# Earlier issue of ScalarE's last weight loads before each mixture-of-experts stage

## The reference

```
g_logits = h @ grp_w + grp_b                    # 4 groups
g_sel    = argmax(g_logits)
e_logits = (h @ exp_w + exp_b)[tok, g_sel]      # 8 experts of that group
e_p, e_i = top_k(softmax(e_logits), 2)
wts      = softmax(g_logits)[g_sel] * e_p / sum(e_p)
...
def run(tok, wt, e):                            # a block of up to 64 tokens of expert e
    xb  = h_pad[tok]
    hid = silu(xb @ w_gate[e]) * (xb @ w_up[e])
    return (hid @ w_down[e]) * wt
out = zeros.at[buf_tok].add(run over all blocks)
```

## Time and profile before

| | us |
|---|---|
| median of 3 runs | 2237.31 |
| lowest and highest run | 2236.52, 2237.57 |
| profiled execution | 2237.01 |
| its span, first to last instruction | 2235.2 |
| TensorE busy in the span | 2043.7 (91%) |
| VectorE, ScalarE, GpSimd busy | 851.1, 400.8, 239.3 |
| moved by DMA | 631.71 MB, mean 283 GB/s |

### The profile page before, as it was taken

One profiled execution on the slowest core, in us unless ns is written; L12 is line 12 of the kernel. 1 busy time (PEld: TensorE's weight loads), 2 busy tenths in 40 slices (PEclk: granted clock), 3 DMA queues, 4 the chain that ended last, 5 costly groups with the idle time before them and its releaser, 6 DMA issues.

```text
span 2235.2 us, 22516 instructions
## 1 busy us (share of the span) xinstructions
PE 2043.7 (91%) x8674; PEld 1067.4 (48%) x8674; DVE 851.1 (38%) x1698; ACT 400.8 (18%) x881; POOL 239.3 (11%) x303
## 2 busy tenths in 40 slices
PE   7989999999999999999988988989688898999985
PEld 3456666444766666445433333334355433434332
DVE  4756773464787126954210110101443311111111
ACT  2241000134100123653000000000343100000001
POOL 2010000000100003310121111111000111111110
PEclk9999999999999999999899999999899899999998
DMA  8865888343788612114899999999745799999996
GB/s 276 228 218 122 299 304 307 132 174 109 257 300 305 217 49 76 76 38 179 314 400 410 398 415 402 392 413 413 264 190 197 303 415 421 381 410 419 415 418 246
DMA packets 130835, 631.71 MB, mean 283 GB/s; under 512 B 16005, under 2 KB 18213, under 8 KB 104385
## 3 DMA queue, kind: packets, MB, share of 16 engines
q1 hardware_dynamic: 108064, 575.10, 65.5%
q0 software_dynamic: 19120, 33.31, 6.1%
q10 hardware_dynamic: 3568, 22.21, 2.6%
HBM read 625.46 MB, written 26.57 MB: 292 GB/s over the span
## 4 chain that ended last, share of the span: by engine, by line
PE 68%; DMA 23%; DVE 5%; ACT 2%; issue 2%; SPq 1%; ACTq 0%; DVEq 0%; POOLq 0%
DMA ring<-ex_up 20%; PE PS L1570 15%; PE PS L1243 10%; PE PS L1232 9%; PE PS L692 6%; PE PS L1170 6%; PE PS L1588 4%; PE PS L595 3%; PE PS L1560 2%; DMA ring<-a_w_qkv 2%; PE PS L2527 2%; PE PS L1028 1%; PE PS L1044 1%; PE PS L1208 1%; PE PS L2558 1%
## 5 line engine op out<-in xcount | busy, mean ns | idle before, releaser
L1570 PE MATMUL PS<-ring,arena 128*64 128x512 f32 x976 | 474.1, 643 | 83.6 <-DMA ring<-ex_up 81.7
L1573 PE MATMUL PS<-ring,arena 128*64 128x512 f32 x992 | 481.8, 643 | 0.0
L1570 PEld LDWEIGHTS PS<-ring,arena 128*64 128x64 f32 x976 | 138.7, 148 | 355.5 <-issue 329.0
L1900 DVE COPY arena<-PS 128x512 f32<-128x512 f32 x64 | 44.3, 692 | 616.3 <-PE PS L1560 616.3
L1588 PE MATMUL PS<-ring,arena 128*64 128x512 f32 x1008 | 230.1, 598 | 1.6 <-DVE arena L1896 1.6
L1243 PE MATMUL PS<-ring,arena 128*128 128x512 f32 x512 | 222.6, 592 | 0.0
L1232 PE MATMUL PS<-arena,ring 128*128 128x256 f32 x896 | 196.9, 380 | 0.0
L1232 PEld LDWEIGHTS PS<-arena,ring 128*128 128x128 f32 x896 | 169.3, 190 | 32.6 <-issue 10.1
L1243 PEld LDWEIGHTS PS<-ring,arena 128*128 128x128 f32 x512 | 97.0, 190 | 115.1 <-issue 114.3
L1702 ACT ACTIVATE arena<-PS 64x512 f32<-64x512 f32 x65 | 38.2, 588 | 610.2 <-PE PS L1570 578.3
L1983 POOL DMA_INDIRECT arena<-tokens_d,arena x65 | 62.4, 959 | 737.1 <-PE PS L1560 553.4
(11 more groups left out here) (317 smaller groups left out, 2245.9 us busy)
## 6 DMA issues: line engine op xcount, KB each, us to landing
ring<-ex_down SPq DMA_DIRECT2D x63, 2048.0 KB, 22.6
ring<-ex_up SPq DMA_DIRECT2D x62, 2048.0 KB, 22.4
ring<-ex_gate SPq DMA_DIRECT2D x61, 2048.0 KB, 17.5
ring<-ffn_w SPq DMA_DIRECT2D x32, 2048.0 KB, 12.9
ring<-mod_w SPq DMA_DIRECT2D x24, 2048.0 KB, 9.9
ring<-a_w_qkv SPq DMA_DIRECT2D x8, 2048.0 KB, 31.5
ring<-b_w_qkv SPq DMA_DIRECT2D x6, 2048.0 KB, 9.8
ring<-w_in_ab SPq DMA_DIRECT2D x3, 2048.0 KB, 8.8
```

The lines of the kernel that those rows point to most:

```text
L1570: g = pe.matmul(PS[0:CAP, u, :], xT[:, k, :], gate[k], start=(k == 0), stop=(k == KD - 1))
L1573: h = pe.matmul(PS[CAP:P, u, :], xT[:, k, :], up[k], start=(k == 0), stop=(k == KD - 1))
```

## The change

ScalarE's load of down_a is issued at the head of `act_moe`, once the logits are done (the turned tokens have been read by then, since ScalarE has copied the last of them). The other loads stay behind the exponents, but wait for the token stores and no longer for the two gathers.

```diff
         def act_moe(act, m, after=None):
             s, b0, T = m.s, m.b, m.tiles
+            act.wait_ge(s.logits, b0.logits + T)
+            spare_load(act, m, "down_a", 0)
             act.wait_ge(s.group_top, b0.group_top + 1)
 ...
             act.sem_inc(s.y_copied, 2)
             for u in range(2):
-                act.wait_ge(s.gathered[u], b0.gathered0 + 16)
-            spare_load(act, m, "down_a", 0)
+                act.wait_ge(s.token_stored[u], b0.token_stored0 + 16 * (T // 2))
             spare_load(act, m, "gate_c", 1)
             if m.l == 0:
                 spare_load(act, m, "gate_a", 1)
```

## The result

The changed kernel takes 2246.18 us (median of 7 runs, 2242.6 to 2252.56), the kernel before 2237.57 (7 runs, 2236.38 to 2239.53). The ratio is 1.0032, with a 95% interval of 1.0017 to 1.0048: slower by some 7 to 9 us. Run once more beside other kernels it gave 2246.30 and a ratio of 1.0040 [1.0024, 1.0057]. The forecast was 2238.1, in a range up to 2242.0. The profiled execution took 2247.5 us with a span of 2245.7; it is one of the slower half, so pieces of it can sum to a little more than the medians differ by.

The account below looks back on a forecast made before the run. The mixtures were taken as bound by DMA bytes, but the time here as set by TensorE's start on expert 0. Bytes, queue and clock at 0 and the first gather's +1.05 us on 2237.01 gave 2238.1 us, range 2235.4 to 2242.0.

Parts of the forecast that it names:

- The bytes: Loads of 3.67 MB and 3.15 MB move into the DMA hole before expert 0; nothing stood behind them: 0 us.
- The first rival: DMA short from the mixture stage's start, so every byte moved into the hole counts: 16.7 us faster, 2220.3 us; chance 0.05.
- ScalarE's queue: down_a's issue moves ahead of the exponents, which end 0.4 us later; later waits cover it: 0 us.
- The first gather: Expert 0's token gather, slowed beside the early loads by 2.05 us: TensorE late by +0.15 and +0.9 us in the layers.
- the slack: Time from the first gather's landing to TensorE wanting it before expert 0: 1.9 us and 1.1 us.
- the halving: Half of the third gather's extra 4.1 us taken for the first gather, as gate_c's packets are 8.3 KB, down_a's 16.3 KB.
- an upper bound of 5.3: First gather takes the third gather's full 7.0 us: TensorE starts 2.2 and 3.1 us late, +5.3 us.
- A gather cannot wait for a queue that is empty: Argument against the slower rival: the early loads' last data end at 1069.8 and 1745.9.
- The clock: TensorE's granted clock around expert 0: its start moves by less than a microsecond, so 0 us.
- My bound of 2.4 us in a layer: Five more pairs of expert 0's gate and up matmuls at the lower clock: +2.4 us in a layer.
- The slower rival: At `tokens_in(0, 0)` in both layers TensorE waits for a first gather of 7.0 us: +5.3 us, 2242.3 us; chance 0.07.

Follow-up runs that it names:

- run 6: Kernel before with the three loads issued only behind the first silu, in the part bound by DMA: 2251.55 us, ratio 1.0065.
- runs 1 and 2: Against the kernel before, only down_a issued early (1: 2240.31 us, ratio 1.0006) or only the gate parts early (2: 2238.22 us, ratio 0.9987).
- Run 8: Kernel before with down_a issued behind the exponents and token stores, the gate parts still behind the first two gathers: 2241.04 us, ratio 1.0021.
- run 11: Changed kernel with 6 keep-awake matmuls instead of 3 ahead of expert 0, and three more in expert 0's two waits: 2240.24 us, ratio 1.0018 to the kernel before.
- run 5: Changed kernel with 6 keep-awake matmuls instead of 3 ahead of expert 0: 2243.52 us, ratio 1.0024 to the kernel before.
- run 12: The whole change measured once more, unaltered, beside the kernel before: 2246.30 us, ratio 1.0040.

## Why the prediction was wrong

*The bytes: right.* They went into the hole, left one behind, and brought nothing. That the bound stretch is dear is shown by run 6 (+14.5 us), and that the old place was free by runs 1 and 2 (no clear gain). The first rival, 2220 us, is out.

*ScalarE's queue: right.* The exponents came 0.5 us later behind the last store in both layers, where I had 0.4, and no wait in these traces goes back to that.

*The first gather: the step that failed.* I had a measured size for it, 4.1 us beside the same three loads, and halved it, because the packets beside it would be half as large. The place, the slack and the direction were right, the halving was not. It landed in 6.4 and 7.2 us instead of 5.0 and 4.9, and TensorE's turn of tokens came 1.6 and 3.3 us late, 4.9 in sum, where I had 1.05 and an upper bound of 5.3. Run 8 shows that the size of the packets was the wrong reason: beside packets twice and more as large, but fewer of them, the delay was smaller. The premise was wrong in the trace before as well. The third gather there, issued at 1073.15, moved its 80 packets from 1077 to 1080, and most of them not beside down_a, as I wrote, but beside the smaller packets of the gate part. Queues in 1077:1078 and 1078:1079:

```profile
q10 hardware_dynamic: 50, 0.30, 72.2%
q0 software_dynamic: 25, 0.04, 10.8%
...
q10 hardware_dynamic: 42, 0.34, 97.3%
q0 software_dynamic: 39, 0.02, 9.7%
```

So 4.1 us was already a value beside packets of 8 KB, with nothing to halve. Taking turns a packet at a time, the Trainium skill's rule in DMA: Bandwidth & Descriptors, section Queues, rings and completion order, would have given 1.6 us; measured are 3.5 and 4.4, and up to 2.9 us behind the issue not one packet of the gather moved. Nor does the third gather of the trace before bear the rule out, as I wrote: with packets of 8 KB it gives 1.6 us there too, against 4.1. For these gathers the measurement decides against the arithmetic that I built on that rule.

*"A gather cannot wait for a queue that is empty": wrong as I used it.* I had the queue empty 3.7 and 3.0 us behind the gather's issue by its mean rate, but its last load landed 7.7 and 7.8 us behind it. The mean of 16 engines hides the tail: in 1070:1071 of the trace after the queue's packets took only 11.7% of the engines' time, and the load was still 1.8 us from landing. Its last three packets moved in 1072:1073.

*The clock: taken as 0, it was 3.9 and 4.7 us in the two traces of the change* (2.8 us by the medians of run 11, roughly). My reason, that a later start only lengthens the wait ahead of the fall, missed that with this wait the clock stayed down longer afterwards: 0.71 and 0.72 on average through expert 0 instead of 0.85, and 0.85 and 1.00 again when run 5 covered the wait. My bound of 2.4 us in a layer held for expert 0 (0.4 to 1.2 us) but not where expert 1 was hit too: 3.5 us in layer 0 of the first trace, 4.0 in layer 1 of run 12. And I held it for a case apart and did not join it to the late gather. They are one chain: late gather, idle TensorE, lower clock, late third load, and DMA with nothing to move until then. The slower rival named this place and this point, 3.7 us of added landing, and both landings came near it or went past it (3.5 and 4.4); I gave it 0.07. Its time, 2242.3 us, was still 4 us short, for want of the clock.

*What I would do now with the same rows:* take the one measured value for a gather beside these loads, 7.0 us, as the likeliest, since nothing nearer was in the trace. That gives 2242.3 us before the clock, and 2244.7 with my own upper bound of 2.4 us for the clock in one layer.

## What to carry to other kernels

Moving a transfer gains nothing where nothing waited behind it; so first look for what stood behind it in its old place. Then look at the short transfer on which the next stage waits, here a gather with 1 to 2 us of slack: look at when whatever is queued ahead of it on the same engines lands, and not at its mean rate. Here a load that landed up to 2.7 us behind the gather's issue cost the gather some 0.6 us at most, one that landed 4.1 to 7.8 us behind cost 1.5 to 4.4. And count to the event that really opens the bound stretch, here the third ring load, two experts on, since a gain or a loss ahead of it may be taken back before it.

## What the runs showed that I had not expected

- The gather beside a full ScalarE queue: 4.3 to 7.2 us to landing in thirteen cases against 2.7 to 2.9 alone, with its first packets, in the trace of the change, some 3 to 4 us behind the issue instead of 1 to 2. What holds them back was not tried and stays open. That the gather waits until the queue runs dry is not the whole of it: the third gather of the kernel before also moved its first packets some 4 us behind its issue, but ScalarE's queue stayed full or nearly so beside it and past it, and it landed 2.3 us ahead of that queue's last load.
- In the kernel before TensorE's clock fell in expert 0, behind a wait of 0.8 us between small matmuls. The fall in expert 1, in the traces of the change, comes at such a wait of 1.5 us. Three keep-awake matmuls in those two waits kept it at 2.4 GHz in both experts and both layers, and made the kernel faster by 3.3 us (ratio 0.9986 [0.9972, 0.9999]), although they are work for nothing. Two of them only moved the fall to the next expert and gained nothing. Why the second fall hits one layer in one execution and the other in the next was not settled.
